# Three moves in the mLSTM stage of a two-layer block: low parts of a weight chunk, the gate products' wait, four transposes

## The chip, the cores and the metric

The kernel runs on one core of a Trainium2 chip. The metric is the device time of one execution in microseconds (us). Before the change it is 2621.66 us, the median of 3 runs (2621.5 to 2622.57 us).

A core has five engines with a queue each, which run side by side and meet only at semaphores: TensorE (PE, matrix products), VectorE (DVE), ScalarE (ACT), GpSimd (POOL) and SyncE (SP, which issues DMA transfers). An instruction that waits for a semaphore holds back everything behind it on its engine.

## The reference, cut to what matters

Two layers over 512 latent and 256 context tokens of width 1024. Layer 0 mixes by convolution and pooling, layer 1 by an mLSTM in both directions; each ends with a mixture of experts. The change lies in the mLSTM layer, in what comes ahead of its scans:

```python
def mlstm_inputs(h, w_in, w_conv, b_conv, w_q, w_k, w_v, w_gates, b_gates):
    u = h @ w_in                                   # 1024 -> 4096
    xm, z = u[..., :MLSTM_E], u[..., MLSTM_E:]     # 2048 each
    xc = silu(dwconv(xm, w_conv, b_conv, (2, 1)))  # 4 taps
    q = blockdiag(xc, w_q)                         # 4x4 blocks
    k = blockdiag(xc, w_k)
    v = blockdiag(xm, w_v)
    g = (concatenate([q, k, v], -1) @ w_gates + b_gates)   # 4 gates x 4 heads
    return heads(q), heads(k) * DH ** -0.5, heads(v), g, sigmoid(z)
```

The gates then go through a log-sigmoid, running sums and running maxima along the tokens (forward and backward), and from these come the weights with which each token's scores are scaled.

## The kernel before, in words

Each engine has a program of its own, written out by hand in the order in which it runs; nothing schedules it. The part around the change runs from about 1350 to 1640 us of the span:

- **xm.** `w_in` is taken in eight chunks of 512 columns. A chunk is loaded raw (`craw`), ScalarE copies it to a rounded high part (`cwh`), and VectorE subtracts to get the low part (`cwl`, line 1865). A product is then three products of parts (`three`: high x high, high x low, low x high). The first four chunks give the 16 channel tiles of xm. TensorE writes tile `ct` into two of the eight PSUM banks, VectorE copies it out (lines 1909, 1910, two increments of `cv_s`) and runs four taps of convolution (1915, 1917), ScalarE applies the silu. The semaphores are `xm_mm` (product done), `cv_s`, `xc_rdy`.
- **z.** The last four chunks give z, only for the latent tokens: 16 products `z`, chunk `z // 4`, token tile `z % 4`, eight steps `k` each (lines 1137 to 1151). Here high and low parts are made per `k`; the first token tile of a chunk waits for each (`c_low`). ScalarE takes the sigmoid of each product (`z_rdy`) and stores it. The raw buffer is loaded again by SyncE when the eight low parts of the chunk before are done (line 570). The loads of the last four slices of modulation weights follow z.
- **Gates.** 64 products with 32 rows of effective gate weights (1154 to 1161) into banks 4 and 5, and two that gather the four partial rows (1164, 1165). VectorE adds the bias, copies out the forget gates (1935, 1937), and goes on with the log-sigmoid (1945), for which ScalarE computes Abs, Exp and Ln, and the scans (1953 to 1955). Each step of this sequence, `row(...)`, waits for the one before it by the semaphore `gr`.
- **Values.** TensorE computes v per head and token tile by block-diagonal matrices `BD[:, 0]` that GpSimd builds (`diagonal`, line 706) when all of z is done. The other two, `BD[:, 1]` and `BD[:, 2]` (k and q), are built when z is stored, and VectorE transposes them in four instructions (1942, `FOLDS` = 4) into `bqk`.
- **Folds.** TensorE multiplies the transposed q and k blocks into one matrix per tile (1185 to 1189), after it has waited for all four transposes (`bt_rdy`). Then it turns the scan rows (1195, 1196), computes 16 tiles of q (1204) and starts the scores.

Of the kernel before, what the change touches and what calls it, by code (L numbers as in the profile page):

```python
# [32 lines left out]
KD = D // P  # L33
# [5 lines left out]
KE = E2 // P  # L39
# [81 lines left out]
def program(nc, x, c, ctx_in, c_ctx, w_ada, b_ada, g_mix, g_ffn, g_final, w_in_ab, w_dw_a, b_dw_a, ln_g_a, ln_b_a,  # L121
# [13 lines left out]
    with es:  # L135
# [6 lines left out]
        def sems(names):  # L142
            return [sem(s) for s in names.split()]
# [33 lines left out]
        def at(off, *dims):  # L177
            n = int(np.prod(dims))
            a = arena[:, off:off + n]
            assert off + n <= AR, (off, dims)  # L180
            if len(dims) == 2:
                a = a.rearrange("p (a b) -> p a b", a=dims[0])
            if len(dims) == 3:
                a = a.rearrange("p (a b c) -> p a b c", a=dims[0], b=dims[1])
            return a
# [32 lines left out]
        for l in range(2):  # L218
# [5 lines left out]
        xm_z, xm_mm, cv_s, xc_rdy, z_mm, z_rdy = sems("xm_z xm_mm cv_s xc_rdy z_mm z_rdy")  # L224
        z_st = sems("z_st0 z_st1")
        raw_in, bd_rdy, bt_rdy, gp_rdy, ge_mm, ge_rdy, g_mm, gr, ga, ar_st, stt_mm, st_rdy = sems(
            "raw_in bd_rdy bt_rdy gp_rdy ge_mm ge_rdy g_mm gr ga ar_st stt_mm st_rdy")
# [106 lines left out]
        BD = at(39024, 3, KE, P)  # L334
# [6 lines left out]
        bqk = at(45168, 2 * KE, P)  # L341
# [450 lines left out]
        def _(pe):  # L792
# [260 lines left out]
            for kind, i, before in AB_ORDER:  # L1053
                if kind in ("value", "gate"):
                    q, g, o = int(kind == "gate"), i // 2, (i % 2) * P
# [14 lines left out]
                if kind == "pool":  # L1070
                    g, o = i // 4, (i % 4) * P
# [3 lines left out]
                else:  # L1075
                    g, q = i // 2, i % 2
# [60 lines left out]
            for z in range(16):  # L1137
                g, i = z // 4, z % 4
# [11 lines left out]
                        ins.then_inc(z_use, 1)  # L1150
                ins.then_inc(z_mm, 1)

            pe.wait_ge(z_rdy, 14)
            for t in range(2 * KE):
                if t < KE:
                    pe.wait_ge(xc_rdy, t + 1)
# [7 lines left out]
            mm(ps[:, 2, 256:512], sel, gpart[:, 0:S_CTX], True, True)  # L1164
            mm(ps[:, 3, :], sel, gpart[:, S_CTX:], True, True).then_inc(g_mm, 1)

            pe.wait_ge(z_rdy, 16)
            for h in range(H):
                for tt in range(NT):
                    n = NT * h + tt  # L1170
# [5 lines left out]
                    for cc in range(HC):  # L1176
                        t = h * HC + cc
# [50 lines left out]
            for u in range(16):  # L1228
                h, i = u // 4, u % 4
# [357 lines left out]
        def _(v):  # L1587
            n = [0]
# [273 lines left out]
            def low(n, what):  # L1862

                v.wait_ge(c_high, n + 1)
                v.tensor_tensor(cwl[what], craw[what], cwh[what].bitcast(F32), ALU.subtract).then_inc(c_low, 1)  # L1865

            def low_slice(ct):
                low(ct, (slice(None), slice(None), slice(ct % 4 * P, ct % 4 * P + P)))

            def low_chunk(g, k):  # L1870
                low(KE + KD * g + k, (slice(None), k, slice(None)))

            v.wait_ge(a_mm, 3)
            turned = ps[:, 6, :].rearrange("p (w h c r) -> p w c h r", w=2, h=2, c=4)
            for h in range(2):
# [25 lines left out]
            for ct in range(KE):  # L1901
                if ct + 4 < KE:
                    low_slice(ct + 4)
                if ct == KE - 1:
                    for k in range(KD):
                        low_chunk(0, k)
                b0 = 2 * (ct % 4) * 512
                v.wait_ge(xm_mm, ct + 1)
                v.tensor_copy(xm[:, ct, 2:2 + S_CTX], psf[:, b0:b0 + S_CTX]).then_inc(cv_s, 1)
                v.tensor_copy(xm[:, ct, 4 + S_CTX:4 + S], psf[:, b0 + S_CTX:b0 + S]).then_inc(cv_s, 1)  # L1910
                for k in range(4):
                    src = xm[:, ct, k:k + XC]
                    v.wait_ge(cv_s, CV_OPS * ct + 2 + k)
                    if k == 0:
                        ins = v.tensor_scalar(xc[:, ct, :], src, par2[:, ct, 0:1], par2[:, ct, 4:5], ALU.mult, ALU.add)
                    else:
                        ins = v.scalar_tensor_tensor(xc[:, ct, :], src, par2[:, ct, k:k + 1], xc[:, ct, :], ALU.mult, ALU.add)
                    ins.then_inc(cv_s, 1)
            for g in range(1, 4):
                for k in range(KD):  # L1920
                    low_chunk(g, k)
            v.wait_ge(z_mm, 16)
            v.wait_ge(g_mm, 1)
            v.tensor_copy(gpart[:, 0:S_CTX], ps[:, 4, 256:512]).then_inc(gp_rdy, 1)
# [3 lines left out]
            def row(ins):  # L1928
                g_n[0] += 1
                ins.then_inc(gr, 1)  # L1930
                v.wait_ge(gr, g_n[0])
# [5 lines left out]
            row(v.tensor_copy(r_lf[0:64, :], G[64:128, :]))  # L1937
            assert g_n[0] == R_F
            row(v.memset(r_zero[0:64, :], 0.0))
            v.wait_ge(bd_rdy, len(ROUNDS) + 2 * KE)  # L1940
            for i in range(FOLDS):
                v.transpose(bqk[:, 8 * i:8 * i + 8].rearrange("p t n -> p (t n)"),
                            BD[:, 1 + i // 2, 8 * (i % 2):8 * (i % 2) + 8].rearrange("p t n -> p (t n)")).then_inc(bt_rdy, 1)
            v.wait_ge(ga, 3)
            row(v.scalar_tensor_tensor(r_lf[0:64, :], r_lf[0:64, :], 0.0, r_x[0:64, :], ALU.min, ALU.subtract))
            row(v.memset(r_x[0:64, :], 1.0))
# [18 lines left out]
            assert g_n[0] == R_X, g_n  # L1965
            row(v.tensor_scalar(r_M[0:64, :], r_M[0:64, :], -1.0, None, ALU.mult))
            assert g_n[0] == R_M, g_n
            v.wait_ge(stt_mm, 1)
            for kind in range(2):
                v.tensor_copy(st[:, kind], ps[:, 6 + kind, 0:256].rearrange("p (i d r) -> p i d r", i=4, d=2)[:, :, :, 0:H]  # L1970
# [160 lines left out]
FOLDS = 4  # L2131
# [31 lines left out]
ROUNDS = [PAIRED[12 * r:12 * r + 12] for r in range(4)]  # L2163
# [23 lines left out]
```

## Time and profile before

| what | value |
|---|---|
| median of 3 runs | 2621.66 us |
| profiled execution, its own time | 2621.5 us |
| its span, first to last instruction | 2619.8 us |
| TensorE busy | 2449.6 us, 94% |
| VectorE busy | 1879.7 us, 72% |
| ScalarE busy | 1318.9 us, 50% |
| GpSimd busy | 278.5 us, 11% |
| mean granted TensorE clock | 0.963 |

The span is the time between the first and the last instruction in the trace; the execution's own time is 1.7 us more. "Busy" adds up the time in which an engine executes. The granted clock is the part of TensorE's full clock (2.4 GHz) that it was given; 0.50 is its lower level, 1.2 GHz. Times in the trace count from the start of the span. The products with the experts' weights fill most of the span; the stretch of the change is some 290 us of it. A matrix product of 32-bit values stands as two records in the trace, one with rounded parts as one.

### The profile page before, as it was taken

Reading aid. Unit: us, or ns where it says so; the run is one execution under the profiler, and the core shown is the slowest. Engines: PE = TensorE matmul, PEld = TensorE weight load, DVE = VectorE, ACT = ScalarE, POOL = GpSimd, SP = SyncE. Lnnn points to the kernel's source line nnn. Section 1 sums busy time; section 2 is a strip of 40 time slices with the busy share of each in tenths; the row PEclk is TensorE's granted clock in tenths of the full one; section 3 lists DMA queues with packets and bytes.
Section 4 is the critical chain, followed back from the end, with each engine's and each line's share of the span. In section 5 each row is a group of like instructions: output and inputs, shape, how many; then the busy total and the mean of one; then the engine's idle time right before and its main releaser. Section 6 shows DMA issues by size and latency. Waiting matters only on the chain.

```text
span 2619.8 us, 29908 instructions
## 1 busy us (share of the span) xinstructions
PE 2449.6 (94%) x10787; PEld 1748.3 (67%) x10787; DVE 1879.7 (72%) x2068; ACT 1318.9 (50%) x1254; POOL 278.5 (11%) x330
## 2 busy tenths in 40 slices
PE   6999989997999999999869999999988999999994
PEld 3555444545888888888558886554446888888883
DVE  2899956447888888888666715555347888889886
ACT  3000103125777777777452323454126777777774
POOL 0535402210000000000100002000000000000001
PEclk8999999997999999999979999999988999999997
DMA  9110266349999999999931233105338999999992
GB/s 337 34 65 33 109 221 184 134 176 378 422 422 395 387 383 379 393 389 387 343 124 65 79 112 130 71 26 181 145 144 360 422 406 384 388 393 381 386 383 109
DMA packets 150261, 671.81 MB, mean 256 GB/s; under 512 B 24826, under 2 KB 34298, under 8 KB 93746
## 3 DMA queue, kind: packets, MB, share of 16 engines
q1 hardware_dynamic: 127554, 591.68, 58.1%
q0 software_dynamic: 20208, 74.98, 7.8%
q10 hardware_dynamic: 2432, 4.26, 0.4%
q8 instruction: 42, 0.69, 0.1%
q14 instruction: 25, 0.20, 0.0%
HBM read 612.59 MB, written 58.29 MB: 256 GB/s over the span
## 4 chain that ended last, share of the span: by engine, by line
PE 88%; DVE 4%; DMA 3%; ACT 2%; issue 1%; POOL 1%; SPq 1%; ACTq 0%; DVEq 0%; POOLq 0%
PE ps L794 84%; PE ps L978 1%; PE ps L984 1%; ACT arena L1256 1%; DMA arena<-in_w_in_ab_dram 1%; PE ps L882 1%; DMA arena<-buf_d,slots 0%; SPq L398 0%; DVE arena L1670 0%; DVE arena L1671 0%; POOL arena L670 0%; PE ps L1236 0%; DMA buf_d<-arena 0%; DMA buf_d<-arena,slots 0%; DVE arena L1689 0%
## 5 line engine op out<-in xcount | busy, mean ns | idle before, releaser
L1795 DVE TENSOR_TENSOR wl<-wx,wh 128x2048 fp32r<-128x2048 f32 x432 | 969.8, 2287 | 49.1 <-ACT wh L1256 48.9
L1256 ACT ACTIVATE wh<-wx 128x2048 fp32r<-128x2048 f32 x432 | 819.5, 1915 | 160.1 <-PE ps L794 143.0
L794 PE MATMUL ps<-arena 128*128 128x512 f32 (+5 forms) x2424 | 799.0, 501 | 18.3 <-ACT arena L1256 10.9
L794 PE MATMUL ps<-wh,xT 128*128 128x512 f32 x2304 | 736.2, 396 | 4.9 <-DVE xT L1812 4.9
L794 PEld LDWEIGHTS ps<-arena 128*128 128x128 f32 (+1 forms) x2424 | 416.1, 188 | 374.2 <-issue 338.0
L794 PEld LDWEIGHTS ps<-wh,xT 128*128 128x128 f32 x2304 | 435.1, 189 | 106.1 <-DVE xT L1812 5.7
L794 PE MATMUL ps<-wl,xT 128*128 128x512 f32 x1152 | 455.4, 395 | 0.0
L1256 ACT ACTIVATE arena<-ps 128x512 f32<-128x512 f32 (+5 forms) x271 | 165.1, 629 | 507.9 <-PE ps L794 369.1
L794 PE MATMUL ps<-wh,gT 128*128 128x512 f32 x1152 | 377.9, 399 | 0.0
L794 PEld LDWEIGHTS ps<-wl,xT 128*128 128x128 f32 x1152 | 217.6, 189 | 47.3
L794 PEld LDWEIGHTS ps<-wh,gT 128*128 128x128 f32 x1152 | 216.8, 188 | 47.2
L1846 DVE SCALAR_TENSOR_TENSOR arena<-arena,par 128x768 f32<-128x768 f32 x232 | 241.1, 1113 | 0.0
L794 PE MATMUL ps<-wl,gT 128*128 128x512 f32 x576 | 226.5, 393 | 0.0
L1256 ACT ACTIVATE arena<-arena 128x1024 f32<-128x1024 f32 (+3 forms) x53 | 50.1, 947 | 296.4 <-DVE arena L1665 151.3
L738 POOL DMA_DIRECT2D buf_d<-arena x36 | 19.3, 537 | 1230.7 <-ACT arena L1256 1230.7
L794 PEld LDWEIGHTS ps<-wl,gT 128*128 128x128 f32 x576 | 108.3, 188 | 22.1
L1865 DVE TENSOR_TENSOR cwl<-craw,cwh 128x512 fp32r<-128x512 f32 (+1 forms) x48 | 39.9, 867 | 88.6 <-ACT cwh L1256 88.6
L1804 DVE TENSOR_TENSOR gT<-ps,gT 128x512 fp32r<-128x512 f32 x72 | 49.5, 688 | 67.7 <-ACT gT L1256 67.7
L1799 DVE TENSOR_TENSOR arena<-arena,ps 128x512 f32<-128x512 f32 x72 | 49.6, 689 | 66.5 <-ACT arena L1256 66.4
L794 PE MATMUL ps<-hTh,cwh 128*128 128x512 f32 (+1 forms) x256 | 88.1, 344 | 8.8 <-DVE hTl L1895 8.8
L1256 ACT ACT_TABLE_LOAD x66 | 84.7, 1283 | 22.5 <-PE ps L794 20.4
L1256 ACT ACTIVATE gT<-ps 128x512 fp32r<-128x512 f32 x72 | 43.1, 599 | 89.6 <-PE ps L984 89.6
(234 smaller groups left out, 1998.0 us busy)
## 6 DMA issues: line engine op xcount, KB each, us to landing
wx<-in_w_dram SPq DMA_DIRECT2D x432, 1024.0 KB, 8.5
arena<-in_w_ada_dram SPq DMA_DIRECT2D x40, 1024.0 KB, 7.6
arena<-buf_d POOLq DMA_DIRECT2D x38, 512.0 KB, 10.7
buf_d<-arena POOLq DMA_DIRECT2D x36, 512.0 KB, 8.0
craw<-in_w_in_c_dram SPq DMA_DIRECT2D x8, 2048.0 KB, 8.8
buf_d<-arena POOLq DMA_DIRECT2D x1, 14848.0 KB, 57.1
arena<-in_w_in_ab_dram SPq DMA_DIRECT2D x8, 1024.0 KB, 12.6
arena<-in_w_out_ab_dram SPq DMA_DIRECT2D x4, 2048.0 KB, 8.8
```

The source lines that it names most:

```text
L738: pool.dma_start(buf_v[:, bass.ds(b + 1, 1), :].rearrange("p a d -> p (a d)"), yy).then_inc(m["yst"], 16)
L794: return pe.matmul(bank_ap, lhsT, rhs, start=first, stop=last)
L882: ins = pe.transpose(ps[:, 4 + k // 4, (k % 4) * P:(k % 4 + 1) * P], part, ident)
L978: ins = pe.transpose(ps[:, 4 + k // 4, (k % 4) * P:(k % 4 + 1) * P], pairs(xg)[:, k // 2, k % 2, :], ident)
L984: ins = pe.transpose(ps[:, q, k * P:(k + 1) * P], pairs(gg)[:, 2 * q + k // 2, k % 2, :], ident)
L1256: return act.activation(out_, in_, f, **kw)
L1795: v.tensor_tensor(wl[:, g], wx[:, g], whs[g % NH].bitcast(F32), ALU.subtract).then_inc(m["low"], 1)
L1799: v.tensor_tensor(gg[:, 512 * q:512 * q + 512], s0[:, 512 * q:512 * q + 512], ps[:, 2 * q + 1, :], ALU.mult).then_inc(m["g"], 1)
L1804: v.tensor_tensor(gTl[:, 4 * q:4 * q + 4, :], ps[:, q, :].rearrange("p (k n) -> p k n", n=P), gTh[:, 4 * q:4 * q + 4, :].bitcast(F32), ALU ...
L1846: ins = v.scalar_tensor_tensor(acc[k % 2], src, w, acc[k % 2], ALU.mult, ALU.add)
L1865: v.tensor_tensor(cwl[what], craw[what], cwh[what].bitcast(F32), ALU.subtract).then_inc(c_low, 1)
```

## The change

Three edits, all in the stretch described above. No instruction of an engine is added or removed; one of the waits goes.

1. On VectorE the eight low parts of z's first chunk, which stood ahead of the evacuation of xm tile 15, now stand behind that tile's convolution, in one run with the other 24.
2. On TensorE the wait ahead of the gate products is for 16 sigmoids of z (all) where it was for 14, and the wait for 16 ahead of the value products is gone.
3. On VectorE the four transposes of the block-diagonal q and k weights, with their wait for GpSimd, now stand behind the scans instead of ahead of the log-sigmoid.

```diff
--- before.py
+++ after.py
@@ -1150,7 +1150,7 @@
                         ins.then_inc(z_use, 1)
                 ins.then_inc(z_mm, 1)
 
-            pe.wait_ge(z_rdy, 14)
+            pe.wait_ge(z_rdy, 16)
             for t in range(2 * KE):
                 if t < KE:
                     pe.wait_ge(xc_rdy, t + 1)
@@ -1164,7 +1164,6 @@
             mm(ps[:, 2, 256:512], sel, gpart[:, 0:S_CTX], True, True)
             mm(ps[:, 3, :], sel, gpart[:, S_CTX:], True, True).then_inc(g_mm, 1)
 
-            pe.wait_ge(z_rdy, 16)
             for h in range(H):
                 for tt in range(NT):
                     n = NT * h + tt
@@ -1867,9 +1866,6 @@
             def low_slice(ct):
                 low(ct, (slice(None), slice(None), slice(ct % 4 * P, ct % 4 * P + P)))
 
-            def low_chunk(g, k):
-                low(KE + KD * g + k, (slice(None), k, slice(None)))
-
             v.wait_ge(a_mm, 3)
             turned = ps[:, 6, :].rearrange("p (w h c r) -> p w c h r", w=2, h=2, c=4)
             for h in range(2):
@@ -1901,9 +1897,6 @@
             for ct in range(KE):
                 if ct + 4 < KE:
                     low_slice(ct + 4)
-                if ct == KE - 1:
-                    for k in range(KD):
-                        low_chunk(0, k)
                 b0 = 2 * (ct % 4) * 512
                 v.wait_ge(xm_mm, ct + 1)
                 v.tensor_copy(xm[:, ct, 2:2 + S_CTX], psf[:, b0:b0 + S_CTX]).then_inc(cv_s, 1)
@@ -1916,9 +1909,8 @@
                     else:
                         ins = v.scalar_tensor_tensor(xc[:, ct, :], src, par2[:, ct, k:k + 1], xc[:, ct, :], ALU.mult, ALU.add)
                     ins.then_inc(cv_s, 1)
-            for g in range(1, 4):
-                for k in range(KD):
-                    low_chunk(g, k)
+            for i in range(4 * KD):
+                low(KE + i, (slice(None), i % KD, slice(None)))
             v.wait_ge(z_mm, 16)
             v.wait_ge(g_mm, 1)
             v.tensor_copy(gpart[:, 0:S_CTX], ps[:, 4, 256:512]).then_inc(gp_rdy, 1)
@@ -1937,10 +1929,6 @@
             row(v.tensor_copy(r_lf[0:64, :], G[64:128, :]))
             assert g_n[0] == R_F
             row(v.memset(r_zero[0:64, :], 0.0))
-            v.wait_ge(bd_rdy, len(ROUNDS) + 2 * KE)
-            for i in range(FOLDS):
-                v.transpose(bqk[:, 8 * i:8 * i + 8].rearrange("p t n -> p (t n)"),
-                            BD[:, 1 + i // 2, 8 * (i % 2):8 * (i % 2) + 8].rearrange("p t n -> p (t n)")).then_inc(bt_rdy, 1)
             v.wait_ge(ga, 3)
             row(v.scalar_tensor_tensor(r_lf[0:64, :], r_lf[0:64, :], 0.0, r_x[0:64, :], ALU.min, ALU.subtract))
             row(v.memset(r_x[0:64, :], 1.0))
@@ -1965,6 +1953,10 @@
             assert g_n[0] == R_X, g_n
             row(v.tensor_scalar(r_M[0:64, :], r_M[0:64, :], -1.0, None, ALU.mult))
             assert g_n[0] == R_M, g_n
+            v.wait_ge(bd_rdy, len(ROUNDS) + 2 * KE)
+            for i in range(FOLDS):
+                v.transpose(bqk[:, 8 * i:8 * i + 8].rearrange("p t n -> p (t n)"),
+                            BD[:, 1 + i // 2, 8 * (i % 2):8 * (i % 2) + 8].rearrange("p t n -> p (t n)")).then_inc(bt_rdy, 1)
             v.wait_ge(stt_mm, 1)
             for kind in range(2):
                 v.tensor_copy(st[:, kind], ps[:, 6 + kind, 0:256].rearrange("p (i d r) -> p i d r", i=4, d=2)[:, :, :, 0:H]
```

VectorE at the end of the xm tiles, before: tiles 14 and 15, with the low parts (line 1865) and the convolutions (1915, 1917).

```order
L1910 COPY arena<-ps 128x512
L1915 TENSOR_SCALAR arena<-arena,par 128x770 [waits cv_s]
L1917 SCALAR_TENSOR_TENSOR arena<-arena,par 128x770 [waits cv_s] x3
L1865 TENSOR_TENSOR cwl<-craw,cwh 128x512 [waits c_high] x8
L1909 COPY arena<-ps 128x256 [waits xm_mm]
L1910 COPY arena<-ps 128x512
L1915 TENSOR_SCALAR arena<-arena,par 128x770 [waits cv_s]
L1917 SCALAR_TENSOR_TENSOR arena<-arena,par 128x770 [waits cv_s] x3
L1865 TENSOR_TENSOR cwl<-craw,cwh 128x512 [waits c_high] x24
```

The same place in the changed kernel, where the lines are numbered 1864 (low part), 1902, 1903 (copies), 1908 and 1910 (convolution).

```order
L1903 COPY arena<-ps 128x512
L1908 TENSOR_SCALAR arena<-arena,par 128x770 [waits cv_s]
L1910 SCALAR_TENSOR_TENSOR arena<-arena,par 128x770 [waits cv_s] x3
L1902 COPY arena<-ps 128x256 [waits xm_mm]
L1903 COPY arena<-ps 128x512
L1908 TENSOR_SCALAR arena<-arena,par 128x770 [waits cv_s]
L1910 SCALAR_TENSOR_TENSOR arena<-arena,par 128x770 [waits cv_s] x3
L1864 TENSOR_TENSOR cwl<-craw,cwh 128x512 [waits c_high] x32
```

The run of eight low parts has gone from between tiles 14 and 15 to behind tile 15 and stands in the 32.

VectorE from the zero row to the end of the first scans, before; the transposes (1942) stand ahead of the log-sigmoid (1945), which waits for ScalarE by `ga`.

```order
L1939 MEMSET arena 64x768 [waits gr]
L1942 STREAM_TRANSPOSE arena<-arena 128x1024 [waits bd_rdy,gr]
L1942 STREAM_TRANSPOSE arena<-arena 128x1024 x3
L1945 SCALAR_TENSOR_TENSOR arena<-arena 64x768 [waits ga]
L1946 MEMSET arena 64x768 [waits gr]
L1958 MEMSET arena 64x768 [waits gr]
L1953 SCALAR_TENSOR_TENSOR arena<-arena 4x768 [waits gr]
L1954 SCALAR_TENSOR_TENSOR arena<-arena 4x256 [waits gr]
L1955 SCALAR_TENSOR_TENSOR arena<-arena 4x512 [waits gr]
L1960 TENSOR_TENSOR arena<-arena 64x768 [waits gr]
```

The changed kernel from the second scans (1941 to 1943) on: the last row (1954), then the transposes (1958) and the copies that wait for TensorE's small transposes.

```order
L1950 MEMSET arena 64x768 [waits gr]
L1941 SCALAR_TENSOR_TENSOR arena<-arena 4x768 [waits gr]
L1942 SCALAR_TENSOR_TENSOR arena<-arena 4x256 [waits gr]
L1943 SCALAR_TENSOR_TENSOR arena<-arena 4x512 [waits gr]
L1952 TENSOR_TENSOR arena<-arena 64x768 [waits gr]
L1954 TENSOR_SCALAR arena<-arena 64x768 [waits gr]
L1958 STREAM_TRANSPOSE arena<-arena 128x1024 [waits bd_rdy,gr]
L1958 STREAM_TRANSPOSE arena<-arena 128x1024 x3
L1962 COPY st<-ps 128x32 [waits stt_mm]
```

The transposes have gone behind the last scan row, immediately ahead of the copies of the turned rows.

## Rows read from the trace of the kernel before

**Rows 1.** The chain that ended last, shares of the span by engine.

```profile
PE 88%; DVE 4%; DMA 3%; ACT 2%; issue 1%; POOL 1%; SPq 1%; ACTq 0%; DVEq 0%; POOLq 0%
```

**Rows 2.** Busy us (and count) of each engine, TensorE clock, DMA, in two stretches.

```profile
1481.00:1580.00 99.00, 98.53 (x508) 77.38 (x512) 24.75 (x38) 30.58 (x51) 8.24 (x23) 1.00 0.39 133
1580.00:1615.00 35.00, 33.87 (x322) 28.59 (x314) 24.82 (x23) 23.93 (x37) 8.98 (x26) 1.00 0.27 100
```

**Rows 3.** ScalarE's timeline: start us, us, engine, line, operation [idle before, its releaser].

```profile
1479.96 4.28 ACT L1256 ACTIVATE cwh<-craw 128x512 fp32r<-128x512 f32 x8 [10.35 <-PE ps L794]
...
1570.49 0.60 ACT L1256 ACTIVATE arena<-ps 128x512 f32<-128x512 f32 x1 [4.94 <-PE ps L794]
...
1588.63 0.60 ACT L1256 ACTIVATE arena<-ps 128x512 f32<-128x512 f32 x1 [0.29 <-PE ps L794]
...
1593.74 0.94 ACT L1256 ACTIVATE arena<-arena,ones 64x768 f32<-64x768 f32 x1
```

**Rows 4.** VectorE's timeline at the end of the xm tiles.

```profile
1468.65 0.42 DVE L1909 COPY arena<-ps 128x256 f32<-128x256 f32 x1
...
1473.47 0.42 DVE L1909 COPY arena<-ps 128x256 f32<-128x256 f32 x1
...
1480.63 4.91 DVE L1865 TENSOR_TENSOR cwl<-craw,cwh 128x512 fp32r<-128x512 f32 x8 [2.25 <-ACT cwh L1256]
```

**Rows 5.** TensorE's timeline: first z product, gate products.

```profile
1481.46 0.47 PE L794 MATMUL ps<-cwh,hTh 128*128 128x512 f32 x1 [1.60 <-DVE cwl L1865]
...
1570.38 10.62 PE L794 MATMUL ps<-arena 128*32 128x256 f32 x128
```

**Rows 6.** The chain in order of time (start us, us, what), 1480 us on.

```profile
1480.63 0.70 DVE cwl L1865
1481.33 0.14 issue
1481.46 99.55 PE ps L794 x512
```

**Rows 7.** VectorE's timeline around the gate rows and the scans.

```profile
1584.40 4.99 DVE L1937 COPY arena<-arena 64x768 f32<-64x768 f32 x1
...
1590.34 4.62 DVE L1942 STREAM_TRANSPOSE arena<-arena 128x1024 f32<-128x1024 f32 x4
1594.89 0.91 DVE L1945 SCALAR_TENSOR_TENSOR arena<-arena 64x768 f32<-64x768 f32 x1
...
1608.16 0.55 DVE L1966 TENSOR_SCALAR arena<-arena 64x768 f32<-64x768 f32 x1
```

**Rows 8.** TensorE's timeline, folds and first small transpose.

```profile
1609.52 3.84 PE L794 MATMUL ps<-arena 128*128 128x128 f32 x32
1613.29 0.27 PE L1195 MATMUL ps<-cst,arena 64*128 64x64 f32 x1
```

**Rows 9.** GpSimd's timeline, the second set of diagonals.

```profile
1577.51 11.46 POOL L706 TENSOR_TENSOR arena<-cst,arena 128x128 f32<-128x128 f32 x32 [1.22 <-DMA zs_d<-arena]
```

**Rows 10.** ScalarE's exponentials and VectorE's first weighing, timeline.

```profile
1620.69 2.00 ACT L1256 ACTIVATE arena<-arena,st 128x256 f32<-128x256 f32 x5 [5.82 <-DMA arena<-arow_d]
...
1634.88 0.56 DVE L1989 SCALAR_TENSOR_TENSOR arena<-ps,arena 128x384 f32<-128x384 f32 x1 [5.70 <-PE ps L794]
```

**Rows 11.** TensorE's timeline, three pauses earlier in the program.

```profile
325.43 1.03 PE L794 MATMUL ps<-arena,scT 128*2 128x256 f32 x8 [5.33 <-DMA arena<-in_w_ada_dram]
...
403.00 25.40 PE L794 MATMUL ps<-arena 128*128 128x512 f32 x52 [3.54 <-ACT arena L1256]
430.99 1.23 PE L882 MATMUL ps<-cst,arena 128*128 128x128 f32 x8 [2.60 <-DVE arena L1690]
```

**Rows 12.** Busy us by engine and TensorE clock, as rows 2, behind each pause.

```profile
325.43:331.50 6.07, 5.48 (x56) 1.42 (x56) 6.03 (x6) 0.00 (x0) 5.68 (x6) 0.61 0.80 283
403.00:410.00 7.00, 7.00 (x10) 3.06 (x11) 6.97 (x10) 4.71 (x9) 0.00 (x0) 0.59 0.00 0
430.99:440.00 9.01, 9.01 (x43) 4.71 (x44) 2.75 (x16) 4.25 (x6) 0.56 (x2) 1.00 1.01 339
```

## The prediction, made before the change was run

> **What bounds the kernel now.** I read the chain of waits on the page first: 88% of the span lies on TensorE [rows 1], so a step costs time only where it makes TensorE stand still or run slower. Then the busy times of the two stages that the change touches: between 1481 and 1580 us TensorE is busy 98.53 of 99 us, between 1580 and 1615 us 33.87 of 35 us, and the granted clock is 1.00, the 2.4 GHz level, in both [rows 2]. There is no slack on TensorE in which a new wait could disappear. Last the timelines of single engines around three joints: from the xm products to the z products (1480 us), from z to the gate products (1570 us), and at the folds (1609 us). The profiled execution took 2621.5 us with a span of 2619.8 us; the median of the runs is 2621.66 us. The sum is made against 2621.5.
>
> **Edit 1, the low parts of weight chunk 0 go behind the convolution of tile 15.** Before, VectorE finishes tile 14, waits for ScalarE's first high part (8 of them from 1479.96 us [rows 3]), starts the eight low parts at 1480.63 us (4.91 us for 8, 0.61 us each) and only then evacuates tile 15, at 1485.5 us [rows 4]. TensorE starts z product 0 at 1481.46 us after 1.60 us of idle time that ends with that low part [rows 5]: 0.70 us for the part and 0.14 us until TensorE runs [rows 6]. Now VectorE meets tile 15 first. It is released by the same last xm product as ScalarE's high parts, so at about 1479.98 us. One tile (two copies, one multiply, three multiply-adds) takes 4.82 us, the distance between the starts of two tiles that follow each other without a wait, 1468.65 and 1473.47 us [rows 4]. So the first low part starts at 1479.98 + 4.82 = 1484.80 us instead of 1480.63: **+4.2 us** on TensorE. Could it be more, the eight chunks now being late one by one? No: z takes 1481.46 to 1570.38 us for 16 x 8 chunk steps [rows 5, 6], 0.69 us a step, and VectorE delivers one in 0.61 us. Less? Only if TensorE waited again later in z for something that did not move, and it is busy 99.5% there. ScalarE has all high parts ready by 1484.24 us, before the first is used. Tile 15 itself is evacuated 5.5 us earlier (1479.98 instead of 1485.5 us), but the products that need its banks or its convolution come 30 us later and more, so this gives nothing back. The next raw chunk is loaded after the eighth low part, about 4.2 us later too, as is everything that uses it. Bounds of this term: 4.1 to 4.3 us.
>
> **Edit 2, z_rdy 16 instead of 14 ahead of the gate products.** z_rdy 16 is the sigmoid of the last z product, which ScalarE runs from 1570.49 to 1571.09 us [rows 3], while TensorE starts the gate products at 1570.38 us [rows 5]. With release they start at 1571.13 us: +0.75 us. Behind the waiting instruction stand all 128 records of the gate (10.62 us) and the value products. The wait that is removed ahead of the value products was met before those 10.62 us were over, so it gives nothing back. The price hides only if something later is late anyway, and that is so in part, as follows.
>
> **Edit 3, four transposes go behind the scans.** VectorE transposes the block-diagonal weights (1590.34 us, 4.62 us for 4) and then goes to the log-sigmoid at 1594.89 us [rows 7]. Its other operand comes from ScalarE, whose Ln runs from 1593.74 to 1594.68 us [rows 3]. So the transposes lie beside ScalarE's work; taking them away saves the scans only 1594.89 - 1594.72 = 0.17 us. Behind the scans nothing covers them. TensorE waits for all four before its first fold: before, it starts the folds at 1609.52 us [rows 8], 14.6 us after the end of the last transpose (1594.96 us), and the records stand without idle time.
>
> Now with edit 2 in it, times without the 4.2 us: GpSimd's diagonals run 1577.51 to 1588.97 us [rows 9]; they hang on z_mm 16 and on the store of z, so edit 2 doesn't move them. VectorE's copy of 64 rows at 1584.40 us takes 4.99 us [rows 7], against 0.55 us for a TENSOR_SCALAR over the same 64x768 elements, and ends at 1589.39 us, 0.4 us after GpSimd's last diagonal. So the copy begins 0.75 us later and ends at about the same time.
> The Trainium skill, "SBUF — State Buffer", section "Terms", at the shared port pair, says that VectorE in a two-port mode and GpSimd take that pair as an exclusive lock and the loser blocks fully. The copy's end just behind GpSimd's last row agrees; by that rule it ends with GpSimd, without it at 1590.14 us, which is 0.2 us more for the sum.
> ScalarE's next step needs the copy and its own last value copy (1588.63 + 0.60 + 0.75 = 1589.98 us [rows 3]) instead of 1589.43 us. That is +0.54 us, so Ln ends at 1595.22 us, the log-sigmoid starts at 1595.26 us, +0.37 us. The last scan row, now at 1608.16 + 0.55 = 1608.71 us [rows 7], ends at 1609.08 us. Then a semaphore (0.04 us), four transposes (4.62 us) and the release of TensorE (0.13 us, as at the first joint [rows 6]): the folds start at 1613.87 us instead of 1609.52, **+4.35 us for edits 2 and 3 together**. The 0.75 us of edit 2 lies inside this, since TensorE is early at the folds. Bounds: 4.2 us (the release is 0.15 us quicker) to 4.6 us (the copy moves fully). Behind the folds the order is as before: the small transposes (1613.29 us [rows 8]) needed the last scan row, which is there. The broadcast of the scan rows lands at 1620.6 us and ScalarE's exponentials are done at 1622.69 us; the first user is VectorE at 1634.88 us [rows 10], so that 12 us of slack take a term of this size and TensorE's later start isn't given back there.
>
> **What the two pauses do to TensorE's clock.** The pauses grow from 1.6 us (no fall: 1.00 around it [rows 2, 5]) to 1485.63 - 1479.86 = 5.8 us at joint 1, and at the folds from none to 1613.87 - (1609.52 + 0.75) = 3.6 us. The trace of before has three pauses of the kind [rows 11]: 5.33 us, with a mean clock of 0.61 in the 6.07 us after it, a loss of 0.39 x 6.07 = 2.4 us; 3.54 us, 0.59 in the 7.00 us after it, a loss of 0.41 x 7.00 = 2.9 us; 2.60 us, with 1.00 after it and no loss [rows 12]. A loss here is time at the 1.2 GHz level in which the work goes half as fast. Both new pauses are longer than the shorter of the two behind which the clock fell, if the second one only by less than 0.1 us, and both stretches behind them are TensorE-bound: z product 0 would take some 1.3 us a chunk step, slower still than VectorE's 0.61. So I take the mean of the two losses, 2.6 us, twice: **+5.2 us**. Bounds: 0 (the pause of 2.60 us) to 2 x 3.5 us; the upper end is an estimate from the same row, its 7.00 us taken as wholly at the lower level. Below nothing it can't be: the clock stands at its upper level already.
> The Trainium skill speaks against this change as well: "TensorE: Matmul & The Clock Gate", section "Why this matters for your kernels", asks that no pauses between bursts of matmuls be left that let the clock fall back. The trace agrees at 3.54 and 5.33 us. Without that rule the sum would be 2630.1 us, with it 2635.3.
>
> **Sum.** 2621.5 + 4.2 + 4.35 + 5.2 = 2635.3 us, +0.5%.
>
> **Rivals.**
> A. The clock falls behind one pause only. The second is the doubtful one. For it: at 3.6 us it lies just above the shortest pause here behind which the clock fell (3.54 us), and one pause of that length is thin evidence. Against it: no pause of that length without a fall is in these rows. 2621.5 + 8.55 + 2.6 = 2632.7 us.
> B. The clock doesn't fall at all: only waits count, 2621.5 + 8.55 = 2630.1 us. For it: pauses up to 2.60 us did nothing. Against it: both that were as long as these did.
> C. The other side: not slower. The scans, not the transposes, would have to be what the rest waits for: then taking 4.62 us of transposes out from before them brings the scan rows, their broadcast and the exponentials forward by up to 4.6 us, and with the 5.5 us that tile 15 gains the change wins. It decides from the point where VectorE's first weighing at 1634.88 us waits for the exponentials (1622.69 us) or the log-sigmoid doesn't wait for ScalarE's Ln. Then 8.55 - 4.6 - 5.5 = -1.5, some 2620 us. Against it stand 12.2 us of slack at the first place and 0.17 us of play at the second.
> D. Two or three small sizes are off in the same direction (the copy moves fully, both losses at 3.5 us): 2621.5 + 4.3 + 4.6 + 7.0 = 2637.4 us. This is the upper edge of the forecast, not a case of its own.
> The change does do what it says: the order of VectorE shows both moves, and the waits are constants.
>
> **How the numbers follow.** Forecast with both falls 0.64 (own range 2633.4 to 2637.4 us, from losses of half the upper bound, 1.75 us each, to D); A 0.19; B 0.12; C 0.02; the rest, 0.03, for an effect that I don't see, near no change. The range goes from B with its lower bounds (2621.5 + 4.1 + 4.2 = 2629.8 us) to just above D, 2637.6 us. A measurement of this kernel can tell about 0.2%, 5.2 us, from no change. All of forecast, A and B lie above 2626.9 us: slower 0.95; within 0.2%: 0.03; faster 0.02.
>
> **What would show it.** Edit 1: idle time of TensorE before z product 0 of about 5.6 us instead of 1.60, released by the low part of the weights, and VectorE with 4 copies and multiplies ahead of it. Edit 2: a pause of 0.7 us ahead of the gate products, released by ScalarE. Edit 3: a pause of 3.6 us ahead of the folds, released by the transposes; the VectorE row of the 64-row copy some 0.7 us shorter than 4.99. The clock: under 0.7 in the 7 us behind each of the two pauses. It would be wrong if the pause before z were under 3 us, if the transposes started before the scans ended, or if the folds had no pause ahead of them.

## The result

| | kernel before | changed kernel |
|---|---|---|
| median, 6 runs each | 2623.22 us | 2636.39 us |
| lowest to highest | 2621.5 to 2625.43 us | 2633.44 to 2638.6 us |
| profiled execution | 2621.5 us | 2634.66 us |
| its span | 2619.8 us | 2633.0 us |
| TensorE busy | 2449.6 us, 94% | 2454.2 us, 93% |
| mean granted clock | 0.963 | 0.961 |

The ratio is 1.0051, with a 95% interval of 1.0041 to 1.0062: 13 us slower (10.8 to 16.3 us). The forecast was 2635.3 us, in a range of 2629.8 to 2637.6 us.

The three joints of the prediction, in the profile of the changed kernel. TensorE at z product 0 [rows 5 of before], and below it the first product at full speed (start us, us, engine, line, operation, idle before and its releaser):

```profile
1485.47 0.76 PE L794 MATMUL ps<-cwh,hTh 128*128 128x512 f32 x1 [5.69 <-DVE cwl L1864]
...
1490.61 0.39 PE L794 MATMUL ps<-cwh,hTh 128*128 128x512 f32 x1
```

The pause has grown from 1.60 to 5.69 us, released by the low part. The twelve products from 1485.47 to 1490.61 us take 5.14 us; in the kernel before, twelve took 2.86 us, from 1481.46 us to this row:

```profile
1484.32 0.39 PE L794 MATMUL ps<-cwh,hTh 128*128 128x512 f32 x1
```

That is 2.3 us more. VectorE ahead of it [rows 4]: tile 15 first, then the low parts (the row shows the first eight), the first at 1484.64 us where 1484.80 was forecast.

```profile
1479.82 0.43 DVE L1902 COPY arena<-ps 128x256 f32<-128x256 f32 x1 [1.74 <-PE ps L794]
...
1481.59 3.13 DVE L1910 SCALAR_TENSOR_TENSOR arena<-arena,par 128x770 f32<-128x770 f32 x3
1484.64 4.90 DVE L1864 TENSOR_TENSOR cwl<-craw,cwh 128x512 fp32r<-128x512 f32 x8
```

ScalarE's last sigmoid, the Abs that follows the 64-row copy, and the Ln [rows 3]:

```profile
1577.59 0.60 ACT L1255 ACTIVATE arena<-ps 128x512 f32<-128x512 f32 x1 [5.00 <-PE ps L794]
...
1596.99 0.83 ACT L1255 ACTIVATE arena<-arena 64x768 f32<-64x768 f32 x1
...
1601.28 0.93 ACT L1255 ACTIVATE arena<-arena,ones 64x768 f32<-64x768 f32 x1
```

GpSimd's second set of diagonals [rows 9]:

```profile
1584.19 11.47 POOL L706 TENSOR_TENSOR arena<-cst,arena 128x128 f32<-128x128 f32 x32 [0.80 <-DMA zs_d<-arena]
```

VectorE's 64-row copy, the log-sigmoid, the last scan row, the transposes and the first weighing [rows 7, 10]:

```profile
1592.26 3.82 DVE L1929 COPY arena<-arena 64x768 f32<-64x768 f32 x1
...
1602.33 0.95 DVE L1933 SCALAR_TENSOR_TENSOR arena<-arena 64x768 f32<-64x768 f32 x1 [5.33 <-ACT arena L1255]
...
1615.63 0.55 DVE L1954 TENSOR_SCALAR arena<-arena 64x768 f32<-64x768 f32 x1
1616.22 4.62 DVE L1958 STREAM_TRANSPOSE arena<-arena 128x1024 f32<-128x1024 f32 x4
...
1649.11 0.56 DVE L1981 SCALAR_TENSOR_TENSOR arena<-ps,arena 128x384 f32<-128x384 f32 x1 [5.70 <-PE ps L794]
```

TensorE at the gate products, the last values, the last slice of modulation and the folds [rows 5, 8]:

```profile
1578.24 10.62 PE L794 MATMUL ps<-arena 128*32 128x256 f32 x128 [0.69 <-ACT arena L1255]
...
1610.85 5.63 PE L794 MATMUL ps<-arena 128*128 128x128 f32 x48
1616.40 1.04 PE L794 MATMUL ps<-arena,scT 128*2 128x256 f32 x16
1620.99 6.66 PE L794 MATMUL ps<-arena 128*128 128x128 f32 x32 [3.54 <-DVE arena L1958]
1627.58 0.27 PE L1194 MATMUL ps<-cst,arena 64*128 64x64 f32 x1
```

The gate products wait 0.69 us for ScalarE, the folds 3.54 us for the transposes, and the folds take 6.66 us instead of 3.84. The clock behind the two long pauses, as in rows 12 (the last figures of a row are the clock, the DMA share and GB/s):

```profile
1485.47:1492.47 7.00, 7.00 (x21) 5.55 (x22) 4.07 (x7) 2.17 (x3) 0.00 (x0) 0.64 0.26 73
1620.99:1628.00 7.01, 7.01 (x38) 6.89 (x39) 0.00 (x0) 2.10 (x4) 0.20 (x1) 0.57 0.70 290
```

Both lie under the 0.7 that was asked of them. Stage by stage, the starts of TensorE's records in the two profiled executions give, after minus before: z product 0 +4.01 us; z, from its first product to the gate products, 92.77 - 88.92 = +3.85 us; gate products 0.00; from the value products to the folds, 31.45 - 27.84 = +3.61 us; from the folds to the q products, 7.69 - 4.93 = +2.76 us; then nothing until VectorE's first weighing; from there to the end 983.89 - 984.92 = -1.03 us. The sum is 13.2 us, as the spans say. "The q products" are the 16 tiles of q that follow the small transposes.

### The profile page after: what moved, and what is told of

Its sections match the earlier page's. It is cut to its first block, busy times and chain, and to the rows that moved or that the text cites. A ratio compares the mean times of both kernels' runs of the same rounds, so it can differ in the third digit from the quotient of the medians.

```text
span 2633.0 us, 29907 instructions
## 1 busy us (share of the span) xinstructions
PE 2454.2 (93%) x10787; PEld 1754.2 (67%) x10787; DVE 1878.3 (71%) x2068; ACT 1318.9 (50%) x1254; POOL 278.6 (11%) x330
## 4 chain that ended last, share of the span: by engine, by line
PE 87%; DVE 5%; DMA 3%; ACT 2%; issue 1%; POOL 1%; SPq 1%; ACTq 0%; DVEq 0%; POOLq 0%
PE ps L794 83%; PE ps L978 1%; ACT arena L1255 1%; PE ps L984 1%; DMA arena<-in_w_in_ab_dram 1%; PE ps L882 1%; DVE arena L1669 0%; DVE arena L1670 0%; SPq L398 0%; DMA arena<-buf_d,slots 0%; POOL arena L670 0%; DMA buf_d<-arena 0%; PE ps L1235 0%; DMA buf_d<-arena,slots 0%; DVE arena L1688 0%
## 5 line engine op out<-in xcount | busy, mean ns | idle before, releaser
L1255 ACT ACTIVATE wh<-wx 128x2048 fp32r<-128x2048 f32 x432 | 819.5, 1915 | 159.8 <-PE ps L794 142.8
## 6 DMA issues: line engine op xcount, KB each, us to landing
arena<-in_w_in_ab_dram SPq DMA_DIRECT2D x8, 1024.0 KB, 12.5
```

The costliest lines, as they stand in the source:

```text
L1255: return act.activation(out_, in_, f, **kw)
```

## The experiments

### The parts one by one

Edit 1 alone, on the kernel before:

```diff
-                if ct == KE - 1:
-                    for k in range(KD):
-                        low_chunk(0, k)
...
-            for g in range(1, 4):
+            for g in range(4):
```

> Edit 1 alone on the kernel before. Theory (waits plus clock): TensorE stands still for 5.7 us before z product 0 instead of 1.60, starts it 4.1 us later, and loses 2.3 to 2.6 us behind that to the lower clock level: +6.4 to +6.8 us, about 2629.5 us on a base of 2623; the folds have no pause. Rival 1 (waits only): +4.1 us. Rival 2 (z runs slower for another reason than the clock, since in the changed kernel z took 3.1 us longer and the lower clock level explains 2.3): +7.2 us, with the last 0.8 us spread over all of z.

Measured: ratio 1.0022 (1.0013 to 1.0031), +5.8 us (3.4 to 8.1 us), which by itself can exclude neither rival. The trace does:

```profile
1487.12 0.77 PE L794 MATMUL ps<-cwh,hTh 128*128 128x512 f32 x1 [5.70 <-DVE cwl L1865]
```

The pause is 5.70 us, and z takes 90.95 us from its first product to the gate products against 88.92: +4.1 and +2.0 us, together 6.1. No pause stands ahead of the folds. The waits alone (rival 1) leave out the 2.0 us, and the extra 0.8 us of rival 2 isn't there in this execution (the repeats below say what it is). The theory holds, with a clock loss 0.3 us under its lower end: the first product at full speed comes 4.4 us behind z product 0, where it was 5.14 us in the changed kernel's profile.

Edit 2 alone:

```diff
-            pe.wait_ge(z_rdy, 14)
+            pe.wait_ge(z_rdy, 16)
...
-            pe.wait_ge(z_rdy, 16)
             for h in range(H):
```

> Edit 2 alone on the kernel before. Theory: a pause of 0.7 us ahead of the gate products and nothing else, +0.75 us, which stays to the end since the folds of this kernel don't wait for VectorE. Rival (the wait is hidden): 0, the 0.7 us missing from a later pause. Both are too small for the times; the positions in the trace decide. VectorE's copy of 64 rows should take 4.2 instead of 4.99 us if it waits for GpSimd.

Measured: ratio 1.0005 (0.9996 to 1.0014), no difference that can be told. The gate products in its trace:

```profile
1571.98 10.61 PE L794 MATMUL ps<-arena 128*32 128x256 f32 x128 [0.69 <-ACT arena L1255]
```

The pause is there and from the value products on every stage is as long as before (27.84 and 4.93 us), so the 0.7 us stays. The stage of z took 90.52 us, 1.6 more than before; 0.85 of it is not this wait (see the repeats below). The copy took 5.32 us, not 4.2: GpSimd had waited 2.26 us for the store of z and ended late, and the copy ended 0.42 us behind it. The next run shows what that can cost.

Edit 3 alone, the `FOLDS` block moved behind `assert g_n[0] == R_M`:

```diff
-            v.wait_ge(bd_rdy, len(ROUNDS) + 2 * KE)
-            for i in range(FOLDS):
-                v.transpose(...).then_inc(bt_rdy, 1)
             v.wait_ge(ga, 3)
...
             assert g_n[0] == R_M, g_n
+            (the same lines)
```

> Edit 3 alone on the kernel before. Theory: the log-sigmoid starts 0.17 us earlier, the four transposes end at 1613.2 us by the clock of the trace of before, the folds start 3.8 us later after a pause of 3.8 us, and the lower clock level costs 2.8 us more behind it: +6.6 us, about 2629.7 us. Rival 1 (waits only): +3.8 us. Rival 2 (earlier scans pay): the rows of the scans come earlier by 4.6 us and the total is +3.8 + 2.8 - 4.6 = +2 us.

Measured: ratio 1.0021 (1.0011 to 1.0031), +5.5 us. The folds, VectorE's copy and GpSimd's diagonals in its trace:

```profile
1616.19 5.64 PE L794 MATMUL ps<-arena 128*128 128x128 f32 x32 [4.97 <-DVE arena L1966]
```

```profile
1586.03 6.11 DVE L1937 COPY arena<-arena 64x768 f32<-64x768 f32 x1
```

```profile
1580.22 11.50 POOL L706 TENSOR_TENSOR arena<-cst,arena 128x128 f32<-128x128 f32 x32 [2.29 <-DMA zs_d<-arena]
```

From the value products to the folds it is 5.04 us more than before, not 3.8, and 1.74 us more for the folds and what follows: 6.8 us in all, the right total by the wrong terms. The scans did not pay anything back (rival 2), and the waits alone are not enough (rival 1). What the expectation missed is the copy: it took 6.11 us, ended at 1592.14 us, 0.42 us after GpSimd's last diagonal, and held ScalarE's Abs back by 1.31 us. GpSimd was late because the store of z had landed late: it waited 2.29 us for it, against 1.22 us in rows 9. That is the execution and not the edit: with the code of before the same wait was 1.22 us in one trace and 1.95 us in another, with the changed code 0.80 and 2.58 us.

Edits 2 and 3 together:

> Edits 2 and 3 on the kernel before, without edit 1. Theory (the wait of edit 2 lies partly inside the pause of edit 3): folds 4.35 us later, clock 2.8 us, +7.15 us, 0.2 us less than the two alone (0.75 + 6.6). Rival 1 (they add): +7.35 us. Rival 2 (they need edit 1): less than 6 us, if the phase in which the pause comes lets the clock stay up.

Measured: ratio 1.0023 (1.0013 to 1.0034), +6.0 us.

```profile
1617.50 5.44 PE L794 MATMUL ps<-arena 128*128 128x128 f32 x32 [3.54 <-DVE arena L1965]
```

0.75 us at the gate products, 31.45 - 27.84 = 3.61 us to the folds, exactly the changed kernel's number, so 4.36 us for the waits where 4.35 was forecast. The clock took 1.54 us here (6.47 us from the folds to the q products instead of 4.93) and 2.76 in the changed kernel; here it was up again before the folds ended. So the theory's overlap of the two waits holds (3.61 us and not 3.8 or 5.04), though this trace and that of edit 3 alone also differ in when GpSimd ended. Its clock term was too large by 1.3 us, so the total came to 5.9 us by the trace, just under the 6 us of rival 2, but not for the reason of rival 2: the clock did fall (a mean of 0.76 in the 7 us behind the pause), only for a shorter time. The interval of the times (3.4 to 8.9 us) tells none of the three apart.

### The clock

The changed kernel with products of constants in the two pauses:

```diff
+            pe.wait_ge(cv_s, CV_OPS * 12 + 2)
+            for _ in range(6):
+                mm(ps[:, 0, :], ones[:], cst[:, 0:512], True, True)
             for z in range(16):
...
             pe.wait_ge(v_ev, NT * H)
+            for _ in range(4):
+                mm(ps[:, 0, :], ones[:], cst[:, 0:512], True, True)
             for i in range(FOLDS):
```

> The changed kernel with products of constants, whose result is overwritten, put into TensorE's two pauses: six (0.86 us each at the full clock) ahead of z product 0, four ahead of the folds. No wait moves; only TensorE's idle time goes. Theory (half of the loss is the clock): the clock stays at 1.00 through z and the folds, z product 0 and the folds start when they did, and 2.3 + 2.8 = 5.1 us come back against the changed kernel: +8.2 to +9 us on the kernel before instead of +13.5. Rival (the slow stretch behind a pause is the pipe refilling, or weights loaded anew): the stretch stays slow and nothing comes back, +13.5 us.

Measured: ratio 1.0029 (1.0018 to 1.0039), +7.6 us (4.7 to 10.2 us) on the kernel before, where the ratio of the changed kernel gives +13.4 (10.8 to 16.3 us). TensorE's timeline with the constants (cst, ones) in the place of the pauses, and the windows behind them:

```profile
1481.49 5.32 PE L794 MATMUL ps<-cst,ones 128*128 128x512 f32 x12
1487.35 0.47 PE L794 MATMUL ps<-cwh,hTh 128*128 128x512 f32 x1 [0.54 <-DVE cwl L1869]
...
1617.01 3.70 PE L794 MATMUL ps<-cst,ones 128*128 128x512 f32 x8
1620.55 3.82 PE L794 MATMUL ps<-arena 128*128 128x128 f32 x32
```

```profile
1487.35:1494.35 7.00, 7.00 (x30) 5.68 (x31) 4.07 (x7) 2.77 (x4) 0.00 (x0) 1.00 0.24 68
1620.55:1627.55 7.00, 6.62 (x46) 5.26 (x46) 1.11 (x4) 2.39 (x4) 0.00 (x0) 1.00 0.70 287
```

The waits are all there: z product 0 starts 5.86 us after the constants begin, the folds 31.38 us after the value products. But the clock is 1.00 behind both, z takes 90.52 us instead of 92.77 (both at the slower of the two speeds that the repeats below show) and the folds with what follows 4.85 instead of 7.69 us. 5.1 us come back by the traces, as the theory said; a pipe that refills or weights that are loaded anew (the rival) would have left the slow stretches as they were. Of the changed kernel's loss, two fifths are the clock and not the waits.

### How long a pause it takes, and the copy

The kernel before with two of the four transposes behind the scans:

```diff
-            for i in range(FOLDS):
+            for i in range(0, FOLDS, 2):
                 v.transpose(...)
...
             assert g_n[0] == R_M, g_n
+            for i in range(1, FOLDS, 2):
+                v.transpose(...)
```

> The kernel before with only the second and fourth of the transposes behind the scans, the first and third where they were. Theory (covered where ScalarE works, exposed behind the scans, and a clock that doesn't fall behind a short pause): two transposes are 2.35 us less behind the scans than four, the folds start 1.5 us later (up to 2.7 if VectorE's copy of 64 rows ends late, as with edit 3 alone), the clock stays at 1.00: +1.5 to +2.7 us, against +6.8 for all four. Rival (cost in proportion): half of 6.8, +3.4 us, with a fall of the clock behind the pause.

Measured: ratio 1.0012 (1.0002 to 1.0021), +3.1 us. The folds; VectorE's copy and first transposes; the clock behind the pause:

```profile
1613.18 5.44 PE L794 MATMUL ps<-arena 128*128 128x128 f32 x32 [2.81 <-DVE arena L1969]
```

```profile
1585.19 6.26 DVE L1937 COPY arena<-arena 64x768 f32<-64x768 f32 x1
1591.67 0.70 DVE L1939 MEMSET arena<- 64x768 f32 x1 [0.22 <-DVE arena L1937]
1592.40 2.37 DVE L1942 STREAM_TRANSPOSE arena<-arena 128x1024 f32<-128x1024 f32 x2
```

```profile
1613.18:1620.18 7.00, 6.61 (x41) 6.13 (x42) 0.29 (x2) 2.46 (x5) 0.09 (x1) 0.76 0.80 341
```

This expectation failed. The copy went on until 1591.45 us, so ScalarE's Abs and with it the scans were late, the pause was 2.81 us, and the clock fell behind it: 2.87 us to the folds and 1.54 us at them, 4.4 us by the trace. The waits came out above even the 2.7 us that a late copy was allowed, and the clock did not stay up. The rival had the fall of the clock right. Its size, half of 6.8 us, was too small by the trace, in which two transposes cost two thirds of what four cost; the interval of the times (0.5 to 5.5 us) holds all these values.

A pause of 2.81 us brought the clock down here; one of 2.60 us did not in rows 11. And the trace of the kernel before has a still shorter pause, which rows 11 leave out, with a lower clock behind it:

```profile
333.71 4.47 PE L794 MATMUL ps<-arena 128*128 128x512 f32 x8 [2.20 <-POOL arena L695]
```

```profile
333.71:341.00 7.29, 6.74 (x48) 3.15 (x48) 7.29 (x9) 1.38 (x2) 0.00 (x0) 0.77 0.79 265
```

The clock was 0.99 in the 2.70 us ahead of this product, which are mostly the pause, and 0.50 in the 2.29 us behind it. It had come up from its lower level shortly before (a mean of 0.63 from 328 to 331 us), so this stretch is not quite like the others. The length of the pause alone doesn't decide whether the clock falls; what does stays open.

Edit 3 alone, with the copy reading PSUM:

```diff
-            row(v.tensor_copy(r_lf[0:64, :], G[64:128, :]))
+            row(v.tensor_scalar(r_lf[0:64, :], psf[64:128, 2 * 512 + 256:4 * 512], gbias[64:128, :], None, ALU.add))
...
-                        pe.wait_ge(gr, R_G)
+                        pe.wait_ge(gr, R_F)
```

> Edit 3 alone, and VectorE's copy of 64 rows (SBUF to SBUF, 6.11 us in the run of edit 3 alone, ended 0.42 us after GpSimd's diagonals) reads PSUM and adds the bias instead; TensorE's wait for bank 2 is for this instruction. Theory (the copy is blocked as long as GpSimd runs its diagonals): the row takes 1.0 us, ScalarE's Abs no longer waits for it, and the pause ahead of the folds falls from 4.97 to 3.6 us. Rival (the copy is slow by itself, or waits for its semaphore): the row stays above 4 us and the pause at about 5.

One execution, 2629.23 us. VectorE's row, ScalarE's last value copy and Abs, and the folds:

```profile
1586.66 1.02 DVE L1937 TENSOR_SCALAR arena<-ps,gbias 64x768 f32<-64x768 f32 x1
```

```profile
1590.89 0.60 ACT L1256 ACTIVATE arena<-ps 128x512 f32<-128x512 f32 x1 [0.29 <-PE ps L794]
1591.38 0.83 ACT L1256 ACTIVATE arena<-arena 64x768 f32<-64x768 f32 x1
```

```profile
1615.39 6.59 PE L794 MATMUL ps<-arena 128*128 128x128 f32 x32 [3.54 <-DVE arena L1966]
```

GpSimd waited 2.24 us for the store of z in this run, nearly as long as with edit 3 alone, and its diagonals ran until 1592.26 us. The row took 1.02 us all the same, Abs followed the value copy at once, and the pause fell from 4.97 to 3.54 us. So the copy was blocked by GpSimd, and its length was a part of the price of edit 3. From the value products to the folds it is 31.45 us here, +3.61 us, as in the changed kernel and with edits 2 and 3: this is what is left when VectorE's row is done before ScalarE's last value copy, which then decides alone when Abs starts. The folds with what follows took 7.63 us here: the clock cost 2.7 us.

### The kernels once more

> The kernel before once more, unchanged, for its trace. In the traces so far z takes either 88.9 us (before, edit 1 alone, the variant with the copy from PSUM) or 89.8 us (all others), less what the low clock level explains. Theory (two speeds that a run falls into, whatever the kernel): this trace may show 89.8 us with the code of before, and VectorE's 64-row copy still ends 0.42 us after GpSimd's diagonals, wherever these end. Rival (the speed belongs to the code): 88.9 us again.

The kernel before took 2624.36 us in this execution. z took 89.76 us (between the starts of the two rows that follow) with the code that took 88.92 us in the profile above, so the two speeds of z belong to the run and not to the code; of the 13.2 us between the two profiles, 0.8 us is this. (The expectation's list of fast ones is one short: the version at the end of this section, with a z of 88.85 us, is another.)

```profile
1484.44 0.47 PE L794 MATMUL ps<-cwh,hTh 128*128 128x512 f32 x1 [1.60 <-DVE cwl L1865]
...
1574.20 10.62 PE L794 MATMUL ps<-arena 128*32 128x256 f32 x128
```

GpSimd's diagonals and VectorE's copy:

```profile
1582.06 11.47 POOL L706 TENSOR_TENSOR arena<-cst,arena 128x128 f32<-128x128 f32 x32 [1.95 <-DMA zs_d<-arena]
```

```profile
1588.22 5.72 DVE L1937 COPY arena<-arena 64x768 f32<-64x768 f32 x1
```

They end at 1593.53 and 1593.94 us. In this kernel the folds start at their usual 27.84 us after the value products, since the transposes and scans have room behind them.

> The changed kernel once more, unchanged, for its trace. Theory: pauses of 5.7 us before z, 0.7 before the gate products and 3.54 before the folds again, the low clock level behind the first and the third, z 89.8 or 88.9 us plus 2.3 us for the clock. If the speed of z belongs to the code, it is 89.8 + 2.3 again.

The changed kernel took 2636.02 us. Pauses of 5.70 us and 0.69 us as forecast, but 4.45 us ahead of the folds:

```profile
1487.92 0.76 PE L794 MATMUL ps<-cwh,hTh 128*128 128x512 f32 x1 [5.70 <-DVE cwl L1864]
...
1623.69 5.44 PE L794 MATMUL ps<-arena 128*128 128x128 f32 x32 [4.45 <-DVE arena L1958]
```

The copy took 5.59 us and GpSimd had waited 2.58 us for the store of z, so the folds came 4.52 us later than before instead of 3.61; the clock took 1.5 us there. z took 92.11 us: 89.76 at the slower of its two speeds, 0.75 for the wait of edit 2, which the expectation left out of its sum, and so 1.6 us for the clock (a mean of 0.75 in the 7 us behind the pause, against 0.64 in the first profile). The expectation's 3.54 us and its 2.3 us for the clock were both too firm: the same kernel lost 5.1 us to the clock in one execution and 3.1 us in the other.

### A version that is faster than both

ScalarE takes the high parts of z's first chunk step by step behind the last xm product, on the kernel before:

```diff
                         ins = three(o, cwh[:, k, cols], cwl[:, k, cols], ...)
+                    if ct == KE - 1 and k < KD - 1:
+                        ins.then_inc(z_use, 1)
...
-                    if g == 0:
-                        act.wait_ge(xm_mm, KE)
-                    elif k < KD - 1:
-                        act.wait_ge(z_use, (KD - 1) * (g - 1) + k + 1)
+                    if k < KD - 1:
+                        act.wait_ge(z_use, (KD - 1) * g + k + 1)
+                    elif g == 0:
+                        act.wait_ge(xm_mm, KE)
```

> Another way with edit 1's place, on the kernel before: ScalarE takes the high part k of z's first chunk as soon as step k of the last xm product is done instead of after the whole product; low parts stay ahead of tile 15. Theory (the joint is bound by the chain last product, high part, low part): the pause of 1.60 us before z product 0 goes nearly, -1.5 us. Rival (the low parts come late anyway since VectorE is busy with tile 14 until 1478.4 us and then with all eight parts): the pause stays over 1 us. Too small for the times, which should show no difference; the trace decides.

Measured: ratio 0.9986 (0.9977 to 0.9995), 3.7 us faster. TensorE's last xm and first z product, and VectorE's low parts:

```profile
1481.34 0.28 PE L794 MATMUL ps<-hTh,cwl 128*128 128x256 f32 x1
1481.45 0.40 PE L794 MATMUL ps<-cwh,hTh 128*128 128x512 f32 x1
```

```profile
1479.35 4.90 DVE L1867 TENSOR_TENSOR cwl<-craw,cwh 128x512 fp32r<-128x512 f32 x8
```

The low parts start directly behind the taps of tile 14 and ahead of the end of xm, and the distance from the last xm product to the first of z is 0.11 us instead of 1.87. That is 1.8 us by the trace; the interval of the times (1.3 to 6.0 us) holds it. (The first z product stands at the same 1481.45 us as before only because xm began and ended 1.7 us later in this execution; between its first and last product xm took 137.24 us, against 137.21 before.) The expectation that the times would show no difference was too careful.

## Why the prediction was right

- **Edit 1, +4.2 us.** Right: 5.69 and 5.70 us of pause in three traces against 1.60, so +4.1 us, and nothing caught up in z. Its reason (VectorE starts tile 15 with the last product, 4.82 us a tile) is in the changed kernel's rows: 1479.82 to 1484.64 us.
- **Edit 2, +0.75 us.** Right as a wait, 0.69 us idle in each trace that has the edit.
- **Edits 2 and 3 together, +4.35 us.** 4.36 us in the profile of the changed kernel and in that of both edits without the first, where ScalarE's last value copy decided when Abs starts, as the prediction had it. In the repeat VectorE's copy decided, and it was 5.27 us. The step ended VectorE's copy with GpSimd's diagonals, which is right in all eleven traces with this copy (0.41 or 0.42 us behind their end), but it took their end as fixed. It hangs on the store of z, for which GpSimd waited 0.80 to 2.58 us. The bound of 4.6 us was therefore too narrow, and that the profile shows 4.36 and not 5.27 us is luck. The copy took 3.82 us where about 4.2 was forecast, because GpSimd was early in that run.
- **The clock, +5.2 us.** The mechanism is shown by the run with constants in the pauses. The size was well met by one execution and less well by the other: 2.3 + 2.8 = 5.1 us in the profile of the changed kernel, 1.6 + 1.5 = 3.1 us in its repeat. Over all traces the loss was 1.6 to 2.3 us behind the pause of 5.7 us (three traces, 2.0 with edit 1 alone) and 1.5 to 2.8 us at the folds (six traces); the forecast of 2.6 us for each pause was at the upper side of both. The narrow margin of rival A (3.6 against 3.54 us) was no danger: in one trace even 2.81 us brought the clock down. The ground of rival B, that pauses up to 2.60 us did nothing, was not what the trace of before shows: the prediction took three of its pauses and left out the one of 2.20 us, behind which the clock was low too.
- **Rivals.** A and B would have shown 2632.7 and 2630.1 us and a clock of 1.00 behind one or both pauses. C is refuted by edits 1 and 3 alone, both slower, and by its own two conditions in the changed kernel: the log-sigmoid waits 5.33 us for ScalarE and the first weighing 5.70 us for TensorE.
- The sum went by one profiled execution at 2621.5 us; the median of the six runs of before is 2623.22 us. The forecast of 13.75 us more meets the 13.2 us between the medians closely. Part of this is luck: the traces give 13.5 us (profile above) and about 12.5 us (repeat) for the change itself, without what a run's own speed in z and the part behind the scans add or take.

## What to carry to other kernels

Price a pause of the busiest engine twice: the wait, and what the clock does behind it. The second is a range, read from every pause of the trace, since here the same pause of 5.7 us cost 1.6 to 2.3 us and one of 3.54 us cost 1.5 to 2.8 us. A step that is free beside another engine's work is not free at the end of a chain, where its whole length is exposed; and a step that shares something with a third engine (here VectorE's copy and GpSimd's diagonals) has no length of its own, so its end has to be followed back to whatever starts that engine. A buffer's refill can be released step by step, and that is worth having where the main engine waits for the refill.

## What was not expected of the hardware

- VectorE's SBUF-to-SBUF copy of 64x768 elements took between 3.82 and 6.26 us in eleven traces, always until 0.41 or 0.42 us after GpSimd's last diagonal, and 1.02 us when the instruction read PSUM. The Trainium skill, "SBUF — State Buffer", section "Terms", calls the pair of ports that the two engines share an exclusive lock, held for the full instruction, and the rows agree. They go further than one instruction: the 32 of GpSimd take 11.46 to 11.51 us, 0.36 us each, so VectorE did not get in between some 9 to 16 of them that followed each other.
- z's 384 products ran in 88.9 us in one execution and 89.8 us in another of the same code, with a granted clock of 1.00 in both. No run here says why.
- The clock's stay at the lower level behind a pause differs from run to run: 1.6, 2.0 and 2.3 us were lost behind pauses of 5.7 us, 1.7 us behind 4.97 us, 1.5 us behind 4.45 us, 1.5 us behind 2.81 us, and 1.5, 2.7 and 2.8 us behind pauses of 3.54 us in three traces. The length of the pause doesn't set the size of the loss.
